# Convolution sums in PSUM, ten adds on GpSimd, and other units cut: a two-layer decoder trunk

## The chip, the cores and the metric

One core of a Trainium2 chip runs the kernel. The metric is the device time of the whole program in microseconds; the median of several executions counts. TensorE multiplies matrices, VectorE (DVE), ScalarE (ACT) and GpSimd (POOL) work element by element, and SyncE (SP) issues DMAs.

## The reference

Two layers on x of 256 tokens by 1024 channels, float32. The first layer, where the change lies:

```python
a, bv, bg, z = jnp.split(h @ w_in, ...)      # 1024, 1024, 1024, 2048 columns
ya = group_matmul(multiscale_pool(a), pool_w) * pool_scale   # windows 2, 4, 8, 16
u = bv * jax.nn.sigmoid(bg)
u = causal_depthwise_conv(u, conv_w, 31 taps) + conv_b
yb = jax.nn.silu(layer_norm(u, cn_g, cn_b))
x = x + (jnp.concatenate([ya, yb], axis=-1) * jax.nn.silu(z)) @ w_out
```

The second layer is attention with 16 heads over the 256 tokens, with per-head norms of queries and keys, and a gated output projection.

## The kernel before

The weights come as 49 units of 1 MiB (128 partitions x 2048 columns), read in order. TensorE takes a unit in one of two ways. A **native** unit is multiplied as it is, in float32. A **split** unit is cut into a high and a low part, and each product becomes three: high by high, low activations, low weights. ScalarE casts the high part (L459, two halves), VectorE subtracts it for the low part (`cut_lo`, L723, two halves). For an **added** unit VectorE does nothing: ScalarE also writes the negated high part (L462), and a GpSimd DMA adds the raw weights to it (`added_low`, L424). Before, units 0, 9, 13, 16, 21, 23 and 25 are native, and 10, 14, 22 and 24 are added.

Units 0 to 7 give gate and value of the convolution in turns, 8 to 11 the four pool groups, 12 to 15 and 17 to 20 the gates z, 16 (`PW`) the pool products with `pool_w`, 21 to 28 the output projection. Units 0 to 15 and 17 to 20 use the PSUM banks 0 to 3 in turn, unit 16 the banks 4 to 7.

The convolution has 31 taps on 8 channel tiles of 256 tokens, taken in four pairs of tiles. A pair's sum stands in `V` in SBUF. ScalarE makes the first tap with the bias (L551). A tap is then either one VectorE operation for each tile (L841, multiply and add), or a **product**: ScalarE multiplies both tiles of the pair (L542, two operations), and VectorE adds the 512 columns (L845). For the first two pairs 14 of the taps go another way (side products): ScalarE multiplies (L518), GpSimd DMAs accumulate in `side_v` (L433), and VectorE adds the two totals at the end (L838).

The order is written out by hand. Each engine's program runs through slots n = 1 to 21; what stands in slot n follows unit n - 1 and prepares the cut of unit n + 2. In VectorE's slot n stand: the gate product of a pair (L876), `cut_lo(n + 2)`, the window sums of pool group n - 9 (L812 to L824), then `taps(n)`. In ScalarE's slot n: the cast of unit n + 2, the products for `taps(n)`, first taps, the gate or copy of unit n, which waits until TensorE has finished it, and side products. The copy of a pool unit (L568) also waits until the window sums before it are done, since they share the buffer `AP`.

Which taps become products, and in which slot, is set by a planner (`conv_plan`). It gives each slot of VectorE and ScalarE 0.95 of a unit's length as time, subtracts the work that is fixed (`slot_work`), and fills the rest with taps. It doesn't know how late an engine really is. Products are kept in a ring of four buffers, and later of four others.

At the end of the first layer the channel mean and the square sum of the layer norm are small matmuls put between output products of unit 23, at `MEAN_AT` and `SUM2_AT` (unit, half, tile). In the second layer ScalarE copies transposed keys and queries out of a bank (`qk_turn_out`, L680), squares them (`qk_squares`, L670), and TensorE transposes the probabilities (`pair_turn`, L1285) into the same bank.

Of the kernel before, what the change touches and what calls it, by code (L numbers as in the profile page):

```python
# [24 lines left out]
S = 256  # L25
# [73 lines left out]
def cut_slot(n):  # L99

    if n == SPARE or n >= Z1[0]:
        return (n - Z1[0]) % 4 if n >= Z1[0] else CUT - 1
    return (cut_index(n) - (n > SPARE) - cut_index(Z1[0]) + 1) % 3

# [6 lines left out]
def slot_free(n):  # L111

    if n == SPARE:
        return released(PW)
# [35 lines left out]
PRODUCTS = 4  # L150
LATE_RING = 4
LATE_SLOT = A[3] + 3

# [5 lines left out]

def side_items(n):  # L160

    return [(pair, n - BG[pair + 1]) for pair in range(SIDE) if 0 <= n - BG[pair + 1] < SIDE_ITEMS]


def product_free(product):

    if product >= LATE_FROM:
        return PRODUCT_USED[product - LATE_RING] if product - LATE_FROM >= LATE_RING else None
    return PRODUCT_USED[product - PRODUCTS] if product >= PRODUCTS else 0


def slot_work(n):

    dve, act = 0, 0.8 * len(side_items(n))
    if n + 2 not in NATIVE and n + 2 not in ADDED and n < OA[0]:
        dve, act = dve + 2.3, act + 1.9
    if n + 3 == SPARE or n + 3 in EARLY_ADDED:
        act += 4.0
    if n - 1 in BV:
        dve, act = dve + 0.6, act + 1.0  # L180
    if n - 1 in A:
        dve += 0.75 * (n - A[0]) + 1.0
    if n - 1 in ZA:
        dve, act = dve + 0.8, act + 0.6
    if n in BG or n in A or n in ZB or n in ZA:
        act += 0.6
    if n in (ZB[0], PW):
        act += 0.7 if n == ZB[0] else 3.2
    return dve, act


def conv_plan():

    plan, last, used, count, before, late, folded = {}, {}, [], 0, None, None, []
    left = {pair: [k for k in range(1, TAPS) if k not in side_taps(pair)] for pair in range(4)}
    folds = [2 * pair + (SIDE_ITEMS + i) % 2 for pair in range(SIDE) for i in range(2)]
    dve_time = act_time = 0.0
    for n in range(BG[1], OA[0] + 1):
# [4 lines left out]
        act_time = min(act_time, ACT_CARRY) + ACT_SHARE * length - act  # L203
        while dve_time > 0 or n == OA[0]:
            here = [pair for pair in left if left[pair] and CONV_PAIRS[pair][0] // 2 < n // 2]
            if not here:
                break
            pair = max(here, key=lambda p: (len(left[p]) - (2 if p == before else 0) - (0 if here == [p] or p < n // 2 - 1 else NEW_LAST), -p))
            before, k, tiles = pair, left[pair].pop(0), CONV_PAIRS[pair]
            if n == LATE_SLOT and late is None:  # L210
                late = len(used)
            free = pair < (n - 1) // 2
            if act_time > 0.8 and free and n < OA[0]:
                count += 1
                plan[n].append((tiles, k, len(used), max(last.get(c, 0) for c in tiles), count))
                used.append(count)
                dve_time, act_time = dve_time - 0.61, act_time - 0.8
# [14 lines left out]
    return plan, last, used, late, folded  # L232
# [3 lines left out]
CONV_PLAN, TILE_DONE, PRODUCT_USED, LATE_FROM, FOLDED = conv_plan()  # L236
# [3 lines left out]
SUM2_AT = 2, 1, 5  # L240
# [3 lines left out]
def hybrid_trunk(nc, xT, w, vec, const, out):  # L244
    with ExitStack() as ctx:
# [100 lines left out]
        first_tap, product_ready, tap = sem("first_tap"), sem("product_ready"), sem("tap")  # L346
        mean_folded = sem("mean_folded")
# [17 lines left out]
        def product_home(product):  # L365

            if product < LATE_FROM:
                b = 2 * (product % PRODUCTS)
                return PR[:, b:b + 2, :]
            i = (product - LATE_FROM) % LATE_RING  # L370
            return (AP, W1, W2)[i][:, :, 0:S] if i < 3 else SG2

        SG2 = SG[:, :].rearrange("p (c t) -> p c t", c=2)

# [32 lines left out]
        def _(pool):  # L407
# [19 lines left out]
            for n in range(BG[1], OA[0]):  # L427
# [7 lines left out]
                if n + 3 in EARLY_ADDED:  # L435
                    added_low(n + 3)
# [13 lines left out]
        def _(act):  # L450
# [70 lines left out]
            for n in range(1, OA[0] + 1):  # L521
# [4 lines left out]
                if n == ZA[0]:  # L526
                    act.wait_ge(tap, PRODUCT_USED[LATE_FROM - 1])
# [6 lines left out]
                for tiles, k, product, _, _ in CONV_PLAN.get(n, ()):  # L534
                    if product is None or k is None:
                        continue
                    if product == LATE_FROM:
# [9 lines left out]
                if n in BG[1:] or n == A[0]:  # L547
                    for c in (n - 2, n - 1):
                        if c == n - 2:
                            act.wait_ge(u_ready, n // 2)  # L550
                        nc.scalar.activation(V[:, c, :], U[:, c, 0:S], ACT.Identity, bias=column(CB + c),  # L551
                                             scale=column(CW + TAPS * c)).then_inc(first_tap, 1)
                if n in BG:
# [5 lines left out]
                for pair, item in side_items(n):  # L559
                    side_product(pair, item)  # L560
                if n in A:
# [14 lines left out]
                if n + 3 in EARLY_ADDED:  # L576
                    cut_hi(n + 3)
# [112 lines left out]
            for octet in range(2):  # L690
                for u, n in enumerate((KU[octet], QU[octet], VU[octet])):
                    for i in range(16):
                        s = 16 * u + i
                        for half in range(2):
                            if s == KT_AT[half]:
# [19 lines left out]
        def _(dve):  # L715
# [111 lines left out]
            def taps(n):  # L827

                for tiles, k, product, ready, _ in CONV_PLAN.get(n, ()):
# [3 lines left out]
                    else:  # L833
                        dve.wait_ge(first_tap, tiles[-1] + 1)
                    if k is None:
                        pair, chain = divmod(product, 2)
                        dve.wait_ge(side_added[pair][chain], 16 * ((SIDE_ITEMS - chain + 1) // 2 - 1))
                        nc.vector.tensor_tensor(V[:, c:c + 2, :], V[:, c:c + 2, :], side_v[:, pair, chain, :, :],  # L838
                                                ALU.add).then_inc(tap, 1)
                    elif product is None:  # L840
                        nc.vector.scalar_tensor_tensor(V[:, c, :], U[:, c, k:k + S], column(CW + TAPS * c + k),  # L841
                                                       V[:, c, :], ALU.mult, ALU.add).then_inc(tap, 1)
                    else:
                        dve.wait_ge(product_ready, product + 1)
                        nc.vector.tensor_tensor(V[:, c:c + 2, :], V[:, c:c + 2, :], product_home(product),  # L845
                                                ALU.add).then_inc(tap, 1)
# [22 lines left out]
            for n in range(1, OA[0] + 1):  # L869
# [9 lines left out]
                if m in A:  # L879
# [7 lines left out]
                taps(n)  # L887
                if n == OA[0]:
                    fold_mean()
                    cut_lo(OA[2], (0,))  # L890
                    centre()
                    cut_lo(OA[2], (1,))
# [4 lines left out]


# [155 lines left out]
        def _(pe):  # L1054
# [102 lines left out]
            for g in range(4):  # L1157
# [3 lines left out]
                if g == 0:  # L1161
                    pe.wait_ge(root_ready, 1)
                for ct in range(2):
# [262 lines left out]
```

## Time and profile before

| | us |
|---|---|
| median of 3 runs | 332.69 (332.54 to 332.81) |
| the profiled execution | 333.14 |
| its span, first to last instruction | 331.3 |

| engine | busy, us | share of the span |
|---|---|---|
| TensorE matmul | 325.0 | 98% |
| VectorE | 256.2 | 77% |
| ScalarE | 230.4 | 70% |
| GpSimd | 51.8 | 16% |

How to read it: busy times are of the whole span. The stretch of the first layer, from 17 to 156 us, is another matter than the mean, and the rows below look into it. TensorE's clock is granted in full in all 40 slices of the page.

### The profile page before, as it was taken

To read this page: it belongs to the slowest core of one execution; us is meant where nothing else is said; L and a number is where in the kernel's file an instruction comes from. 1 tells how busy PE (TensorE), PEld (TensorE's weight loads), DVE (VectorE), ACT (ScalarE), POOL (GpSimd) and SP (SyncE) were. 2 spreads that over 40 slices of the span, in tenths; PEclk is the share of its full clock that TensorE was granted. 3 is DMA by queue.
4 is the path that set the end of the run, shared out by engine and by line. 5 is a ranking of instruction groups with operands and counts; after the bars stand their busy time and mean duration, and the time that the engine had idled before them with its cause. 6 is when DMAs were issued, how large, how long until landed. Compare 5 with 4: busy or idle time off the path is not lost.

```text
span 331.3 us, 5760 instructions
## 1 busy us (share of the span) xinstructions
PE 325.0 (98%) x2212; PEld 296.2 (89%) x2212; DVE 256.2 (77%) x475; ACT 230.4 (70%) x429; POOL 51.8 (16%) x58
## 2 busy tenths in 40 slices
PE   8999999999999999999999999999999999999995
PEld 8899999999989999997999999988887776778885
DVE  2699989999689999996886898747556877748633
ACT  4677999994999897935775557824756666575630
POOL 0050024424422310120000000005500231400000
PEclk9999999999999999999999999999999999999999
DMA  7979488979999998676629343780634323200003
GB/s 277 409 272 357 146 267 217 202 164 349 276 252 345 167 380 296 130 174 208 254 103 403 130 133 133 279 347 10 245 127 166 135 99 132 108 0 2 2 0 127
DMA packets 12842, 64.77 MB, mean 195 GB/s; under 512 B 1424, under 2 KB 1552, under 8 KB 6544
## 3 DMA queue, kind: packets, MB, share of 16 engines
q1 hardware_dynamic: 8064, 53.78, 43.2%
q0 software_dynamic: 4608, 10.49, 17.3%
q8 instruction: 17, 0.28, 0.3%
q10 hardware_dynamic: 144, 0.15, 0.2%
q14 instruction: 9, 0.07, 0.1%
HBM read 52.88 MB, written 1.05 MB: 163 GB/s over the span
## 4 chain that ended last, share of the span: by engine, by line
PE 93%; DMA 3%; ACT 1%; DVE 1%; issue 1%; POOL 0%; ACTq 0%; POOLq 0%
PE bank L1058 25%; PE bank L1060 23%; PE bank L1059 23%; PE bank L1118 5%; PE bank L1092 4%; DMA w_lo<-raw 3%; PE bank L1166 2%; PE bank L1272 2%; PE bank L1299 2%; PE bank L1135 2%; PE bank L1126 2%; PE bank L1285 2%; PE bank L1251 1%; ACT scratch L467 1%; DVE scratch L752 1%
## 5 line engine op out<-in xcount | busy, mean ns | idle before, releaser
L723 DVE TENSOR_TENSOR w_lo<-raw,w_hi 128x1024 fp32r<-128x1024 f32 x76 | 90.3, 1222 | 19.6 <-ACT w_hi L459 19.4
L1058 PE MATMUL bank<-h_hi,w_hi 128*128 128x256 f32 x304 | 86.6, 285 | 0.4 <-DMA w_lo<-raw 0.4
L459 ACT CAST w_hi<-raw 128x1024 fp32r<-128x1024 f32 x84 | 84.4, 1048 | 2.7 <-PE bank L1060 2.7
L1060 PE MATMUL bank<-h_hi,w_lo 128*128 128x256 f32 x304 | 86.0, 283 | 0.0
L1059 PE MATMUL bank<-h_lo,w_hi 128*128 128x256 f32 x304 | 86.0, 283 | 0.0
L1058 PEld LDWEIGHTS bank<-h_hi,w_hi 128*128 128x128 f32 x304 | 58.3, 192 | 0.9 <-issue 0.8
L1059 PEld LDWEIGHTS bank<-h_lo,w_hi 128*128 128x128 f32 x304 | 58.3, 192 | 0.1
L1060 PEld LDWEIGHTS bank<-h_hi,w_lo 128*128 128x128 f32 x304 | 58.3, 192 | 0.0
L841 DVE SCALAR_TENSOR_TENSOR scratch<-scratch,params 128x256 f32<-128x256 f32 x108 | 44.1, 484 | 0.2
L1058 PE MATMUL bank<-w_hi,h_hi 128*128 128x512 f32 x96 | 39.2, 408 | 0.0
L1058 PE MATMUL bank<-ya_hi,w_hi 128*128 128x256 f32 x128 | 38.1, 297 | 0.0
L1060 PE MATMUL bank<-w_hi,h_lo 128*128 128x512 f32 x96 | 37.6, 391 | 0.0
L1059 PE MATMUL bank<-w_lo,h_hi 128*128 128x512 f32 x96 | 37.5, 391 | 0.0
L1060 PE MATMUL bank<-ya_hi,w_lo 128*128 128x256 f32 x128 | 36.1, 282 | 0.0
L1059 PE MATMUL bank<-ya_lo,w_hi 128*128 128x256 f32 x128 | 36.1, 282 | 0.0
L433 POOL DMA_DIRECT2D side_v<-side_ring x24 | 21.1, 908 | 70.8 <-ACT side_ring L518 65.7
L542 ACT ACTIVATE scratch<-scratch,params 128x256 f32<-128x256 f32 x76 | 31.9, 505 | 0.0
L845 DVE TENSOR_TENSOR scratch<-scratch 128x512 f32<-128x512 f32 x38 | 25.7, 692 | 1.4 <-ACT scratch L542 0.2
L1058 PEld LDWEIGHTS bank<-ya_hi,w_hi 128*128 128x128 f32 x128 | 24.4, 191 | 2.0 <-issue 1.7
L1059 PEld LDWEIGHTS bank<-ya_lo,w_hi 128*128 128x128 f32 x128 | 24.5, 191 | 0.1
L1060 PEld LDWEIGHTS bank<-ya_hi,w_lo 128*128 128x128 f32 x128 | 24.4, 191 | 0.0
L444 POOL TENSOR_SCALAR scratch<-scratch 128x8 f32<-128x8 f32 x8 | 4.3, 535 | 122.1 <-DVE scratch L1018 121.9
(106 smaller groups left out, 549.0 us busy)
## 6 DMA issues: line engine op xcount, KB each, us to landing
raw<-w SPq DMA_DIRECT2D x49, 1024.0 KB, 6.3
side_v<-side_ring POOLq DMA_DIRECT2D x24, 256.0 KB, 8.2
w_lo<-raw POOLq DMA_DIRECT2D x8, 512.0 KB, 8.1
X<-xT SPq DMA_DIRECT2D x2, 512.0 KB, 5.2
out<-X SPq DMA_DIRECT2D x4, 256.0 KB, 2.6
consts<-const SPq DMA_DIRECT2D x1, 290.0 KB, 13.5
params<-vec ACTq DMA_DIRECT2D x1, 149.0 KB, 4.9
```

What stands on the lines that cost most here:

```text
L433: pool.dma_start(side_v[:, pair, item % 2, :, :], side_home(pair, item), accum_op=ALU.add).then_inc(side_added[pair][item % 2], 16)
L459: nc.scalar.copy(halves(w_hi, cut_slot(n), half), halves(raw, n % RAW, half)).then_inc(hi_cut, 1)
L542: last = nc.scalar.mul(product_home(product)[:, i, :], U[:, c, k:k + S], column(CW + TAPS * c + k))
L723: nc.vector.tensor_tensor(halves(w_lo, cut_slot(n), half), halves(raw, n % RAW, half), halves(w_hi, cut_slot(n), half).bitcast(F32), ALU.s ...
L841: nc.vector.scalar_tensor_tensor(V[:, c, :], U[:, c, k:k + S], column(CW + TAPS * c + k), V[:, c, :], ALU.mult, ALU.add).then_inc(tap, 1)
L845: nc.vector.tensor_tensor(V[:, c:c + 2, :], V[:, c:c + 2, :], product_home(product), ALU.add).then_inc(tap, 1)
L1058: nc.tensor.matmul(dst, wh, ah, start=start, stop=False, skip_group_check=True)
L1059: nc.tensor.matmul(dst, wh, al, start=False, stop=False, skip_group_check=True)
L1060: return nc.tensor.matmul(dst, wl, ah, start=False, stop=stop, skip_group_check=True)
L1092: last = nc.tensor.matmul(dst, wr, (H if n else H0)[:, k, :], start=start, stop=stop, skip_group_check=True)
L1118: return nc.tensor.matmul(dst, wr, SZ[:, (KD if n in OB else 0) + tile, :], start=start and m % 2 == 0, stop=stop, skip_group_check=True)
L1126: nc.tensor.matmul(bank[7][:, 0:P], ones[:, :], ones[:, :], start=True, stop=True, skip_group_check=True)
```

## The change

- Unit 9 becomes split; it was native. Units 10 and 14 become plain split units, cut by VectorE; they were added. Unit 12 becomes an added unit. With four buffers for cut weights in use from the start (`SLOT_ORDER`), the buffers of the units up to 12 are given out anew.
- VectorE's sums for slots up to 15 stand in PSUM, in banks 4 to 7 (`partial`), not in `V`. ScalarE's first taps go there too.
- GpSimd has sums of its own in `V`. ScalarE starts each of the four with one tap (in slots 3, 5, 7 and 11) and makes ten products for GpSimd, which adds them (`pool_conv`) in its slots 4, 6, 8, 13 and 14, behind a wait for the cut of that slot (`pool_gate`), none in the slots of the pool units.
- In slot 15, behind `cut_lo(17)`, four VectorE adds merge the sums of the banks with those in `V`. TensorE waits for them ahead of unit 16 (`MERGED`). From there on VectorE's sums stand in `V`.
- The products for VectorE fall from 38 to 23, in other ring buffers (`RINGS`), while single taps are 110 for 108.
- In slot 10 the window sums come after the taps; in slot 9 ScalarE makes the added cut of unit 12 ahead of its copy.
- The square sum of the layer norm stands one tile later, `centre` comes after the last low part, and in the second layer ScalarE copies the second half of the keys out before its second square, not after it.

```diff
-NATIVE = frozenset((0, 9, 13, 16, 21, 23, 25))
-EARLY_ADDED = (10, 14)
+NATIVE = frozenset((0, 13, 16, 21, 23, 25))
+EARLY_ADDED = (12,)
...
+FOUR, SLOT_ORDER = ZA[1], (3, 2, 0, 1)
...
-PRODUCTS = 4
-LATE_RING = 4
+RINGS = (0, (1, 2, 3)), (A[0], (2, 3)), (A[1], (3, 4)), (ZB[0], (4,)), (ZB[1], (4, 5, 6, 7))
...
+MERGE_SLOT = PW - 1
...
+POOL_ADDS = {4: (0, 0), 6: (0, 1), 8: (1, 2), 13: (2,), 14: (2, 3, 3)}
+POOL_STARTS = {3: (0,), 5: (1,), 7: (2,), 11: (3,)}
...
+def pool_gate(n):
+
+    if n - 1 in A:
+        return "pooled", n - A[0]
+    return ("cut", 2 * low_cuts(n + 2) + 2) if n + 2 not in NATIVE and n + 2 not in ADDED else None
...
+        for pair in range(4) if n == MERGE_SLOT else ():
+            tiles = CONV_PAIRS[pair]
+            count += 1
+            plan[n].append((tiles, None, None, max(last[c] for c in tiles), count))
...
-SUM2_AT = 2, 1, 5
+SUM2_AT = 2, 1, 6
...
+        def partial(tiles):
+
+            c = tiles[0]
+            at = S * (c % 2)
+            t = bank[4 + c // 2][:, at:at + S * len(tiles)]
+            return t.rearrange("p (c t) -> p c t", c=2) if len(tiles) == 2 else t
...
+            def pool_conv(n):
+
+                gate = pool_gate(n)
+                if gate and POOL_PLAN[n - 1]:
+                    pool.wait_ge(pooled if gate[0] == "pooled" else lo_cut, gate[1])
+                for pair, k, made, ready, _ in POOL_PLAN[n - 1]:
+                    if ready:
+                        pool.wait_ge(pool_tap, ready)
+                    else:
+                        pool.wait_ge(pool_started, 2 * pair + 2)
+                    pool.wait_ge(pool_product, made)
+                    nc.gpsimd.tensor_tensor(V[:, 2 * pair:2 * pair + 2, :], V[:, 2 * pair:2 * pair + 2, :],
+                                            pool_home(made), ALU.add).then_inc(pool_tap, 1)
...
-                    if product_free(product):
-                        act.wait_ge(tap, product_free(product))
+                    if FREE_AT[product]:
+                        act.wait_ge(tap, FREE_AT[product])
...
-                        nc.scalar.activation(V[:, c, :], U[:, c, 0:S], ACT.Identity, bias=column(CB + c),
+                        nc.scalar.activation(partial((c,)), U[:, c, 0:S], ACT.Identity, bias=column(CB + c),
...
                 for t in range(TT):
+                    if isq and t and KT_AT[1] == 32:
+                        qk_turn_out(octet, 0, 1)
...
+                    total = partial(tiles) if done <= MERGED else V[:, c:c + 2, :] if len(tiles) == 2 else V[:, c, :]
+                    if k is None and product is None:
+                        dve.wait_ge(pool_tap, POOL_LAST[c // 2])
+                        nc.vector.tensor_tensor(V[:, c:c + 2, :], total, V[:, c:c + 2, :], ALU.add).then_inc(tap, 1)
...
-                if m in A:
+                if m in A and n + 2 not in EARLY_ADDED:
                     window_sums(m - A[0])
...
                 taps(n)
+                if m in A and n + 2 in EARLY_ADDED:
+                    window_sums(m - A[0])
...
                 if g == 0:
                     pe.wait_ge(root_ready, 1)
+                    pe.wait_ge(tap, MERGED)
```

## Rows read from the trace of the kernel before

**Rows 1.** The page, part 1: engine, busy us (share), instructions; then PEld, DVE, ACT.

```profile
PE 325.0 (98%) x2212; PEld 296.2 (89%) x2212; DVE 256.2 (77%) x475; ACT 230.4 (70%) x429; POOL 51.8 (16%) x58
```

**Rows 2.** TensorE's waits, whole span: waiter, releaser: us in total, times, longest.

```profile
PE bank L1285 <- issue: 0.6, 1, 0.6
PE bank L1135 <- DVE scratch L752: 0.5, 1, 0.5
PE bank L1058 <- DMA w_lo<-raw: 0.4, 1, 0.4
```

**Rows 3.** Chain of waits in order of time: start us, us, what.

```profile
10.30 6.91 PE bank L1092 x32
63.28 6.91 PE bank L1092 x32
...
94.78 0.36 PE bank L1058
106.52 6.91 PE bank L1166 x32
```

**Rows 4.** Timeline of VectorE: start us, us, line, operation, count.

```profile
60.26 0.69 DVE L876 TENSOR_TENSOR scratch<-bank,scratch 128x512 f32<-128x512 f32 x1
...
74.61 1.44 DVE L812 TENSOR_TENSOR scratch<-scratch 128x540 f32<-128x540 f32 x2
...
83.25 2.94 DVE L812 TENSOR_TENSOR scratch<-scratch 128x540 f32<-128x540 f32 x4
...
104.95 2.36 DVE L723 TENSOR_TENSOR w_lo<-raw,w_hi 128x1024 fp32r<-128x1024 f32 x2
...
119.90 1.90 DVE L845 TENSOR_TENSOR scratch<-scratch 128x512 f32<-128x512 f32 x3
...
128.98 4.06 DVE L841 SCALAR_TENSOR_TENSOR scratch<-scratch,params 128x256 f32<-128x256 f32 x10
```

**Rows 5.** Timeline of VectorE: the low parts of units 26 to 28.

```profile
168.86 6.90 DVE L723 TENSOR_TENSOR w_lo<-raw,w_hi 128x1024 fp32r<-128x1024 f32 x6 [0.25 <-ACT w_hi L459]
```

**Rows 6.** Timelines of ScalarE and TensorE in the second layer; idle before, and releaser.

```profile
280.48 0.60 ACT L670 ACTIVATE scratch<-bank 128x512 f32<-128x512 f32 x1 [1.46 <-DVE scratch L1018]
...
281.90 0.85 PE L1285 MATMUL bank<-consts,scratch 128*128 128x128 f32 x6 [0.64 <-issue]
```

**Rows 7.** Groups by shape, 20 to 160 us: busy us, mean ns; idle before.

```profile
L841 DVE SCALAR_TENSOR_TENSOR scratch<-scratch,params 128x256 f32<-128x256 f32 x108 | 44.1, 484 | 0.2
L845 DVE TENSOR_TENSOR scratch<-scratch 128x512 f32<-128x512 f32 x38 | 25.7, 692 | 1.4 <-ACT scratch L542 0.2
L876 DVE TENSOR_TENSOR scratch<-bank,scratch 128x512 f32<-128x512 f32 x4 | 2.8, 688 | 0.0
...
L542 ACT ACTIVATE scratch<-scratch,params 128x256 f32<-128x256 f32 x76 | 31.9, 505 | 0.0
```

**Rows 8.** Timeline of ScalarE: start us, us, line, operation, count, idle before.

```profile
77.14 0.59 ACT L568 COPY scratch<-bank 128x512 f32<-128x512 f32 x1 [2.02 <-DVE scratch L824]
...
81.73 0.59 ACT L568 COPY scratch<-bank 128x512 f32<-128x512 f32 x1 [2.41 <-PE bank L1060]
...
98.56 3.30 ACT L542 ACTIVATE scratch<-scratch,params 128x256 f32<-128x256 f32 x8
...
103.84 1.99 ACT L459 CAST w_hi<-raw 128x1024 fp32r<-128x1024 f32 x2
```

**Rows 9.** Timelines of GpSimd and VectorE.

```profile
17.59 4.55 POOL L415 TENSOR_TENSOR qscale<-consts,params 128x8 f32<-128x8 f32 x1 [16.29 <-DMA consts<-const]
...
280.47 0.24 POOL L444 TENSOR_SCALAR scratch<-scratch 128x8 f32<-128x8 f32 x1 [12.31 <-DVE scratch L1018]
...
283.24 1.16 POOL L444 TENSOR_SCALAR scratch<-scratch 128x8 f32<-128x8 f32 x1 [0.78 <-DVE scratch L1018]
...
283.08 1.23 DVE L723 TENSOR_TENSOR w_lo<-raw,w_hi 128x1024 fp32r<-128x1024 f32 x1
```

**Rows 10.** Busy us by window: stretch, length, PE, PEld, DVE, ACT, POOL; PEclk, DMA, GB/s.

```profile
94.78:100.54 5.76, 5.76 (x48) 5.76 (x49) 5.72 (x13) 5.76 (x15) 1.75 (x2) 1.00 1.06 304
```

More of the change, by code:

```diff
@@ L113, in slot_free @@
     if n == SPARE:
-        return released(PW)
+        return released(max(m for m in CUTS if m <= FOUR and cut_slot(m) == CUT - 1))
     if n == Z1[3]:
@@ L149, with pool_products @@
 SIDE_ITEMS = 14
-PRODUCTS = 4
-LATE_RING = 4
+RINGS = (0, (1, 2, 3)), (A[0], (2, 3)), (A[1], (3, 4)), (ZB[0], (4,)), (ZB[1], (4, 5, 6, 7))
 LATE_SLOT = A[3] + 3
+MERGE_SLOT = PW - 1
+POOL_ADDS = {4: (0, 0), 6: (0, 1), 8: (1, 2), 13: (2,), 14: (2, 3, 3)}
+POOL_STARTS = {3: (0,), 5: (1,), 7: (2,), 11: (3,)}
+def pool_products():
+    plan, starts, taken, count, made, last = {}, {}, {pair: 0 for pair in range(4)}, 0, 0, {}
+    for n in range(BG[1], MERGE_SLOT + 1):
+        for pair in POOL_STARTS.get(n, ()):
+            starts[n] = starts.get(n, ()) + ((pair, FIRST_POOL[pair]),)
+            taken[pair], last[pair] = taken[pair] + 1, 0
+        plan[n - 1] = []
+        for pair in POOL_ADDS.get(n, ()):
+            made, count = made + 1, count + 1
+            plan[n - 1].append((pair, FIRST_POOL[pair] - taken[pair], made, last[pair], count))
+            taken[pair], last[pair] = taken[pair] + 1, count
+    return plan, starts, taken, last
 def side_taps(pair):
     return range(TAPS - SIDE_ITEMS, TAPS) if pair < SIDE else ()
+FIRST_POOL = [TAPS - 1 - (SIDE_ITEMS if pair < SIDE else 0) for pair in range(4)]
+POOL_PLAN, POOL_START, POOL_TAKEN, POOL_LAST = pool_products()
+POOL_USED = [done for items in POOL_PLAN.values() for _, _, _, _, done in items]
+def pool_gate(n):
+    if n - 1 in A:
+        return "pooled", n - A[0]
+    return ("cut", 2 * low_cuts(n + 2) + 2) if n + 2 not in NATIVE and n + 2 not in ADDED else None
 def side_items(n):
     return [(pair, n - BG[pair + 1]) for pair in range(SIDE) if 0 <= n - BG[pair + 1] < SIDE_ITEMS]
[L165 to L169, printed above, removed]
 def slot_work(n):
@@ L192, in conv_plan @@
 def conv_plan():
-    plan, last, used, count, before, late, folded = {}, {}, [], 0, None, None, []
-    left = {pair: [k for k in range(1, TAPS) if k not in side_taps(pair)] for pair in range(4)}
+    plan, last, used, count, before, late, folded, homes, free_at = {}, {}, [], 0, None, None, [], [], []
+    left = {pair: list(range(1, FIRST_POOL[pair] - POOL_TAKEN[pair] + 1)) for pair in range(4)}
     folds = [2 * pair + (SIDE_ITEMS + i) % 2 for pair in range(SIDE) for i in range(2)]
@@ L203, in conv_plan @@
         act_time = min(act_time, ACT_CARRY) + ACT_SHARE * length - act
+        for pair in range(4) if n == MERGE_SLOT else ():
+            tiles = CONV_PAIRS[pair]
+            count += 1
+            plan[n].append((tiles, None, None, max(last[c] for c in tiles), count))
+            dve_time -= 0.61
+            last.update({c: count for c in tiles})
+        if n == MERGE_SLOT:
+            merged = count
         while dve_time > 0 or n == OA[0]:
@@ L216, in conv_plan @@
                 used.append(count)
+                ring = next(homes for first, homes in reversed(RINGS) if n >= first)
+                homes.append(ring[len(homes) % len(ring)])
+                free_at.append(max([u for u, h in zip(used[:-1], homes[:-1]) if h == homes[-1]], default=0))
                 dve_time, act_time = dve_time - 0.61, act_time - 0.8
@@ L231, in conv_plan @@
             last.update({c: count for c in tiles})
-    return plan, last, used, late, folded
+    return plan, last, used, late, folded, merged, homes, free_at
 DVE_SHARE, ACT_SHARE, NEW_LAST, ACT_CARRY = 0.95, 0.95, 40, 1.0
-CONV_PLAN, TILE_DONE, PRODUCT_USED, LATE_FROM, FOLDED = conv_plan()
+CONV_PLAN, TILE_DONE, PRODUCT_USED, LATE_FROM, FOLDED, MERGED, HOMES, FREE_AT = conv_plan()
 MEAN_AT = 2, 0, 1
-SUM2_AT = 2, 1, 5
+SUM2_AT = 2, 1, 6
 EARLY = (BG[0],), (Z1[0], Z1[1])
@@ L425, in added_low, with side_sums @@
                                    accum_op=ALU.add).then_inc(lo_added[i][half], 16)
-            for n in range(BG[1], OA[0]):
+            def side_sums(n):
                 for pair, item in side_items(n):
@@ L526, in _ @@
                 if n == ZA[0]:
-                    act.wait_ge(tap, PRODUCT_USED[LATE_FROM - 1])
+                    act.wait_ge(tap, max(MERGED, PRODUCT_USED[LATE_FROM - 1]))
                 if n - 1 in ZA:
@@ L827, in taps @@
             def taps(n):
-                for tiles, k, product, ready, _ in CONV_PLAN.get(n, ()):
+                for tiles, k, product, ready, done in CONV_PLAN.get(n, ()):
                     c = tiles[0]
```

68 lines of the change are left out of this document (45 added, 23 removed).

## The prediction, made before the change was timed

> **What bounds the kernel now.** I read the busy table first: TensorE is busy for 98% of the span [rows 1], so this kernel ends when TensorE ends, and a change counts only by what it does to TensorE's queue. The waits of TensorE come next: after its start they are 0.6 us ahead of the transposes of L1285, 0.5 us for a square sum and 0.4 us for a low half brought by a GpSimd DMA [rows 2]. Then the chain of waits in order of time: unit 0, native, takes 6.91 us from 10.30; units 1 to 8, split, end at 63.28, which is (63.28 - 17.21) / 8 = 5.76 us each; native unit 9 takes 6.91 again; unit 14 starts at 94.78 and the pool product (unit 16) 2 x 5.76 = 11.52 later, at 106.30 (its row begins at 106.52) [rows 3]. Last, the timelines of VectorE and ScalarE, for how far each runs behind TensorE. VectorE cuts unit 17's low half, the first step of its slot 15, from 104.95 [rows 4]; slot 15 opens when unit 14 is done, at 100.54. So VectorE is 4.4 us late there, which costs nothing before: unit 17 is read only at 106.3 + 6.91 = 113.2.
>
> **What the change takes off TensorE.** Unit 9 split instead of native: 6.91 - 5.76 = 1.15 us less. Unit 14 plain: its DMA wait of 0.42 goes. The square sum one output tile later: of the 0.5 us wait [rows 2] one native product (6.91 / 16 = 0.43) is put in the place. But VectorE starts the low half of unit 26 at 168.86, and the first of its two parts is done 1.2 later, at 170.1 [rows 5]; TensorE asks for it at about 170.3. Being 0.43 earlier against this chain, it would wait some 0.2. I count 0.25. The keys' second copy out (L680) moves ahead of the second square: today ScalarE stands idle 1.46 us before that square and copies after it, and TensorE waits 0.64 for the bank [rows 6]. The two copies (0.40 each, below) fit into the idle time; I count 0.6. Together 2.4 us, as long as nothing new waits.
>
> **Sums of the other engines.** Durations, from start to start: VectorE's 128x256 tap 0.396 ((4.06 - 0.484) / 9), a 512-wide add 0.605 ((1.90 - 0.692) / 2), a cut of one unit 2.3; ScalarE's product half 0.40 ((3.30 - 0.505) / 7) and cast of one unit 1.9 [rows 4, 7, 8]. Walking the plan through both programs gives for VectorE: cuts +4 halves (9, 10, 14 in, 12 out), +4.6; single taps 108 to 110, +0.8; product adds 38 to 23, -9.1; four merges, +2.4: in all 1.3 us less. ScalarE: casts +2 halves, negations -2, product halves 76 to 46, and 20 for GpSimd, and 8 that start its sums: -0.8. Both look relieved. But these sums hide a deadline.
>
> **The new deadline.** VectorE's sums now stand in banks 4 to 7, which unit 16 overwrites. So TensorE waits for the four merges; they stand in slot 15 behind the cut of unit 17. With no earlier stall TensorE reaches unit 16 at 106.30 - 1.15 - 0.42 = 104.7. Slot 15 opens at 98.97, and cut and merges take 2.3 + 2.5 = 4.8 of its 5.76 us: VectorE may be 1 us late there, not 4.4. Behind the waiting matmul stands all the rest of TensorE's queue.
>
> I walk the two queues to that point. Up to slot 7 VectorE loses six adds (-3.6), gets two taps (+0.8), unit 9's cut (+2.3) and 0.8 of waiting for that unit's high half: it starts slot 8 (the gate product, L876) at 60.4 instead of 60.26 [rows 4]. Slot 8: 0.6 + cut 2.3 + 8 taps 3.2, to 66.4. Slot 9: cut 2.3, window sums of pool group 0 1.6, 2 taps 0.8, to 71.1. Slot 10 has no cut any more, but its 8 taps (3.2) stand ahead of the window sums of group 1 (about 2.35, from 74.61 to the copy that they release at 77.14 [rows 4, 8]), which end at 76.7. The copy of unit 10 on ScalarE waits for them, as before, and comes at 76.75 instead of 77.14. (A level of window sums is 2.94 / 4 = 0.73 [rows 4]; hence 1.6 for group 0, 3.1 for group 2, 3.85 for group 3.)
>
> Slot 11 is where it turns. Products 2 and 4 share a buffer. VectorE does the window sums of group 2 first, from 77.4 to 80.5, so product 2 is added by 81.2, and ScalarE can make product 4 only then, where its queue would have had it 2.4 us earlier. It goes on: product 0.8, start of the fourth GpSimd sum 0.8, side products 1.6, and the copy of unit 11 at 84.45. Before, that copy came at 81.73, right behind TensorE [rows 8]. From there ScalarE is never idle: before, its slot 14 products end 101.86 - 81.73 = 20.1 us after this copy [rows 8]; the change takes two negations (2.1) and two products (1.6) out of this stretch, which leaves 16.4: the last product is ready at 100.8, those before it at 0.8 steps. VectorE has by then done cut 14, window sums of group 3 (to 92.1), cut 15 and 8 taps (97.6), so it follows the products: 101.4, 8 taps 104.6, cut of unit 17 106.9, four merges **109.4**. ScalarE's cast of unit 17 starts near 102.8 (103.84 before [rows 8]), in time.
>
> TensorE therefore idles from 104.7 to 109.4, 4.7 us, and unit 16 starts 109.4 - 106.3 = 3.1 us later than before; the 1.15 and 0.42 are inside that difference. Between slot 9 and the merges the two queues wait for TensorE nowhere on this walk, so a late DMA for unit 12 (needed at 80.5) would only move TensorE's idle time. On SyncE's queue the reloads of the raw buffers of units 9 and 10 now wait for VectorE's cuts at 57 and 63, earlier than for the native product's end at 70.2, and the reload for unit 17 waits for unit 13 as before; I count nothing for them. Behind unit 16 ScalarE and VectorE follow TensorE as before, 3.1 us later. Sum: 3.1 - 0.25 - 0.6 = +2.25. From the profiled execution, 333.14 (span 331.3 and 1.8 around it), that is 335.4; it lies 0.45 above the median of 332.69, so **334.9**.
>
> **GpSimd.** No row shows a wide add there. From below it is VectorE's 0.69 [rows 7], from above the 4.55 of its 8-wide product [rows 9]; I take 1.2 to 2, nearer to the lower end, since its 8-wide L444 alone needs only 0.24 [rows 9]. The same L444 takes 1.16 when it falls under a VectorE cut, and ends 0.09 after that cut [rows 9]. So a cut holds GpSimd. The ten adds are gated behind the slot's cut and run beside taps. The last three follow the side DMAs of slot 13, from about 98.7, and the last merge needs them at 108.8: they decide from 3.3 us each. On this walk they cost nothing.
> The Trainium skill (SBUF — State Buffer, "SBUF: two separate sides") lets GpSimd and a VectorE operation with two SBUF inputs lock each other out of a shared port pair, which speaks for sums in PSUM. The 1.16 us row agrees for the one direction.
>
> **VectorE on PSUM.** Its reads cost nothing: 0.688 with a bank as input, 0.692 without [rows 7]. Writes to a bank are in no row. From below: taps as much as 0.1 us faster, which would save 0.8 of the stall in slot 14. From above: each operation holds its successor until it has ended, 0.484 + 0.02 instead of 0.396, 0.11 each; 31 of them lie on the walk (18 up to the window sums of group 1, 13 from the last product), +3.4. I take nothing, by the nearest row.
> The Trainium skill (VectorE: DVE Perf Modes, "The TRN2 errata") gives an operation with its source in PSUM 62 cycles more, 65 ns at 0.96 GHz as an estimate. By it the sum would be 2.0 us higher, 336.9; the 0.688 us row speaks against it.
>
> **The rivals.** (A) The forecast, with TensorE waiting 3.1 to 6.2 us at unit 16: 333.4 to 336.5; 0.50. (B) *Faster*: the relief of 1.3 us and the earlier casts act at once, and the merges are done by 104.7; 332.69 - 2.4 = 330.3. It decides where the walk is 4.7 us too slow. For it: both engines' sums fall. Against: in the 5.76 us from 94.78 VectorE is busy for 5.72 and ScalarE for 5.76 [rows 10], so there is no idle time to take up. 0.17. (C) Product 4 doesn't hold ScalarE in slot 11: the walk is 2.4 shorter, 332.5, no change. The order of the code speaks against it. 0.10. (D) Bank writes hold their successors: +2 to +3.4, 336.9 to 338.3; 0.08. (E) TensorE's granted clock falls in the idle 4.7 us. It is 1.00 [rows 10], the level of 2.4 GHz, in every slice of the page, but the longest wait behind the start is 0.64 [rows 2, 6], so no row tests this. At 1.2 GHz the work behind it takes double; if that holds for a third to a half of unit 16's 6.91, +2.3 to +3.4, about 337.5; 0.12. (F) The change doesn't do what it says, since GpSimd's adds take 4.5 us: 98.7 + 13.6 + 0.7 = 113.0 instead of 109.4, +3.6, 338.5; 0.03.
> On (E) the Trainium skill (TensorE: Matmul & The Clock Gate, "What's actually happening") says that an idle array falls to the lower clock.
>
> **The numbers.** A measurement can tell 0.2% from no change: 332.0 to 333.4. Slower: A 0.50, D 0.08, E 0.12, F 0.03, together 0.73. Same: C, 0.10. Faster: B, 0.17. A's own range is 333.4 to 336.5; to hold 8 in 10 the range takes in C below, and E and most of D above: 331.9 to 338.0. B and F are outside.
>
> **What would show it.** The waits of TensorE led by one of 4.7 us ahead of the pool product, released by a VectorE add; the four merges as one row from about 106.9; the copy of unit 11 near 84.5, behind a ScalarE wait in slot 11; unit 9 at 5.76; no wait ahead of the transposes near 281; GpSimd adds of 1.2 to 2 us; taps at 0.40 from start to start. The prediction is wrong if the merges start before 102.5, or if TensorE's wait is there and something before it made up for it.

## The result, and the profile after

The changed kernel takes 337.40 us (median; 337.22 to 337.83), the kernel before 332.73. The ratio is 1.0141, with a 95% interval of 1.0128 to 1.0154: 4.7 us slower. Direction and place were as forecast, the size was twice the forecast 2.25.

The page of the changed kernel, to be read beside [rows 1]: the line of busy times in tenths and that of the granted clock, 40 slices of 8.4 us each.

```profile
span 335.6 us, 5803 instructions
...
PE   8999999999994999999999999999999999999995
...
PEclk9999999999998799999999999999999999999999
...
L810 DVE TENSOR_TENSOR w_lo<-raw,w_hi 128x1024 fp32r<-128x1024 f32 x80 | 94.9, 1220 | 25.1 <-ACT w_hi L534 24.9
```

TensorE has a hole in slice 13, and behind it, in slices 13 and 14, its clock is granted at 8 and 7 tenths. Before, both lines were full. The span grew by 4.3.

TensorE's waits, over the whole span, against [rows 2]:

```profile
PE bank L1258 <- DVE scratch L925: 4.2, 1, 4.2
PE bank L1217 <- POOL eps L461: 1.0, 1, 1.0
PE bank L1226 <- ACT scratch L542: 0.4, 1, 0.4
PE bank L1149 <- DVE w_lo L810: 0.3, 1, 0.3
PE bank L1149 <- DMA w_lo<-raw: 0.3, 1, 0.3
```

L1258 is the pool product (unit 16), L925 a merge: the new wait is 4.2 us. The wait ahead of the transposes (0.6) is gone, and so is that for the layer norm's square sum (the 0.4 at L1226 is at the start). The DMA that TensorE waits for is now unit 12's, and the 0.3 released by a VectorE cut (L810) is the low part of unit 26.

The chain of waits in order of time, against [rows 3]: start us, us, what.

```profile
9.76 6.91 PE bank L1183 x32
...
104.13 0.81 ACT scratch L617 x2
105.14 1.22 DVE w_lo L810
106.36 2.40 DVE scratch L925 x4
108.90 9.57 PE bank L1258 x32
```

From unit 0 to unit 16 it is 108.90 - 9.76 = 99.1 us, where [rows 3] have 106.3 - 10.3 = 96.0: 3.1 more. And unit 16 itself takes 9.57, not 6.91: 2.66 more. (This execution starts unit 0 half a microsecond earlier, at 9.76. To compare its times below with those of the kernel before, add 0.54.) The two together are 5.76; less the 1.0 that the change saves behind unit 16 (measured alone further down) that is 4.8, against the measured 4.7.

Busy times of TensorE by windows of 2 us: stretch, length, busy (matmuls), granted clock, DMA share, GB/s.

```profile
102.00:104.00 2.00, 2.00 (x19) 1.00 1.03 313
104.00:106.00 2.00, 0.69 (x6) 1.00 1.09 207
106.00:108.00 2.00, 0.00 (x0) 0.75 1.14 210
108.00:110.00 2.00, 1.10 (x3) 0.50 1.07 187
110.00:112.00 2.00, 2.00 (x6) 0.50 0.52 91
112.00:114.00 2.00, 2.00 (x7) 0.55 0.55 95
114.00:116.00 2.00, 2.00 (x11) 1.00 0.22 36
```

TensorE stops at 104.7. During the wait the clock falls to 0.50, the lower of its two levels, 1.2 GHz. It stays there for 5 us of work, in which 6 or 7 matmuls end in 2 us instead of 11, and comes back near 114.

The timelines of VectorE and ScalarE up to there, against [rows 4] and [rows 8]:

```profile
76.77 2.20 DVE L899 TENSOR_TENSOR scratch<-scratch 128x540 f32<-128x540 f32 x3 [0.71 <-ACT scratch L655]
...
97.87 3.10 DVE L935 TENSOR_TENSOR bank<-bank,scratch 128x512 f32<-128x512 f32 x4 [0.80 <-ACT scratch L617]
100.88 3.22 DVE L931 SCALAR_TENSOR_TENSOR bank<-scratch,params,bank 128x256 f32<-128x256 f32 x8
104.00 2.35 DVE L810 TENSOR_TENSOR w_lo<-raw,w_hi 128x1024 fp32r<-128x1024 f32 x2
106.28 2.47 DVE L925 TENSOR_TENSOR scratch<-bank,scratch 128x512 f32<-128x512 f32 x4
```

```profile
76.15 0.59 ACT L655 COPY scratch<-bank 128x512 f32<-128x512 f32 x1 [2.21 <-DVE scratch L911]
76.63 1.71 ACT L617 ACTIVATE scratch<-scratch,params 128x256 f32<-128x256 f32 x4
80.61 0.91 ACT L617 ACTIVATE scratch<-scratch,params 128x256 f32<-128x256 f32 x2 [2.27 <-DVE bank L935]
...
83.83 0.56 ACT L655 COPY scratch<-bank 128x512 f32<-128x512 f32 x1
```

ScalarE makes two products at 76.63, waits 2.27 for VectorE to take the first out of the shared buffer, and makes the third at 80.61; the copy of unit 11 follows at 83.83. VectorE gets the products of slot 14 from 97.87, cuts unit 17 at 104.00 and merges from 106.28.

### The profile page after: what moved, and what is told of

Read it like the earlier page. It is cut to its first block, busy times and chain, and to the rows that moved or that the text cites. A ratio compares the mean times of both kernels' runs of the same rounds, so it can differ in the third digit from the quotient of the medians.

```text
span 335.6 us, 5803 instructions
## 1 busy us (share of the span) xinstructions
PE 325.5 (97%) x2228; PEld 296.8 (88%) x2228; DVE 253.4 (76%) x470; ACT 229.2 (68%) x427; POOL 62.3 (19%) x66
## 4 chain that ended last, share of the span: by engine, by line
PE 74%; DVE 12%; ACT 10%; DMA 1%; issue 1%; ACTq 0%; DVEq 0%
PE bank L1149 20%; PE bank L1151 19%; PE bank L1150 19%; DVE bank L931 3%; PE bank L1258 3%; DVE w_lo L810 3%; ACT side_ring L593 2%; PE bank L1209 2%; ACT w_hi L534 2%; PE bank L1183 2%; PE bank L1364 2%; PE bank L1391 2%; PE bank L1226 2%; PE bank L1377 2%; DMA X<-xT 1%; ACT scratch L617 1%
## 5 line engine op out<-in xcount | busy, mean ns | idle before, releaser
L810 DVE TENSOR_TENSOR w_lo<-raw,w_hi 128x1024 fp32r<-128x1024 f32 x80 | 94.9, 1220 | 25.1 <-ACT w_hi L534 24.9
L1149 PE MATMUL bank<-h_hi,w_hi 128*128 128x256 f32 x320 | 91.2, 285 | 0.3 <-DMA w_lo<-raw 0.3
L1150 PE MATMUL bank<-h_lo,w_hi 128*128 128x256 f32 x320 | 90.5, 283 | 0.0
L1151 PE MATMUL bank<-h_hi,w_lo 128*128 128x256 f32 x320 | 90.5, 283 | 0.0
L1149 PEld LDWEIGHTS bank<-h_hi,w_hi 128*128 128x128 f32 x320 | 61.4, 192 | 0.5 <-issue 0.4
L1150 PEld LDWEIGHTS bank<-h_lo,w_hi 128*128 128x128 f32 x320 | 61.4, 192 | 0.1
L1151 PEld LDWEIGHTS bank<-h_hi,w_lo 128*128 128x128 f32 x320 | 61.4, 192 | 0.0
L931 DVE SCALAR_TENSOR_TENSOR bank<-scratch,params,bank 128x256 f32<-128x256 f32 x76 | 30.8, 482 | 0.1
L1149 PEld LDWEIGHTS bank<-w_hi,h_hi 128*128 128x128 f32 x96 | 18.0, 188 | 5.6 <-issue 2.3
L1209 PE MATMUL bank<-scratch,raw 128*128 128x256 f32 x96 | 21.5, 379 | 0.0
```

What stands on the lines that cost most here:

```text
L810: nc.vector.tensor_tensor(halves(w_lo, cut_slot(n), half), halves(raw, n % RAW, half), halves(w_hi, cut_slot(n), half).bitcast(F32), ALU.s ...
L931: nc.vector.scalar_tensor_tensor(total, U[:, c, k:k + S], column(CW + TAPS * c + k), total, ALU.mult, ALU.add).then_inc(tap, 1)
L1149: nc.tensor.matmul(dst, wh, ah, start=start, stop=False, skip_group_check=True)
L1150: nc.tensor.matmul(dst, wh, al, start=False, stop=False, skip_group_check=True)
L1151: return nc.tensor.matmul(dst, wl, ah, start=False, stop=stop, skip_group_check=True)
L1209: return nc.tensor.matmul(dst, wr, SZ[:, (KD if n in OB else 0) + tile, :], start=start and m % 2 == 0, stop=stop, skip_group_check=True)
```

## The experiments

The theory after the result has three parts: the merges come late because both queues lag (unit 16 starts 3.1 us later than before); the lag's last 2.3 us come from the shared product buffer; and the idle wait costs a second time, since TensorE's clock falls. Times are medians; each ratio is to the kernel before on the same chip.

### Is it the clock that makes unit 16 longer?

```diff
                 if g == 0:
                     pe.wait_ge(root_ready, 1)
+                    pe.wait_ge(sz_ready, 1)
+                    for _ in range(9):
+                        nc.tensor.matmul(bank[0][:, 0:S], ones[:, :], H0[:, 0, :], start=True, stop=True,
+                                         skip_group_check=True)
                     pe.wait_ge(tap, MERGED)
```

> The changed kernel with nine extra native products (about 3.9 us of TensorE work, result not used) into bank 0 inside TensorE's 4.2 us wait ahead of unit 16. Theory (clock): the 2.7 us that unit 16 takes over its 6.91 come from the granted clock, which fell during the idle wait; kept busy, TensorE runs unit 16 in 6.9 us at a clock of 1.00, and the time falls by 2.7, from 337.4 to 334.7. Rival (something else slows unit 16, such as VectorE and ScalarE at PSUM beside it or the reading of the weights): unit 16 still takes 9.6 us and the time stays at 337.4. In both the wait for the merges ends at the same moment, near 108.9.

Measured: 335.03 us (334.89 to 335.08), ratio 1.0074 (1.0059 to 1.0089). Its timeline of TensorE:

```profile
105.25 4.05 PE L1256 MATMUL bank<-scratch,ones 128*128 128x256 f32 x18
109.13 7.07 PE L1262 MATMUL bank<-scratch,raw 128*128 128x256 f32 x32
```

Its chain of waits has unit 16 as

```profile
109.30 6.91 PE bank L1262 x32
```

More work for TensorE, and 2.4 us less time. Its clock is 1.00 in every window from 102 to 116, and unit 16 takes 6.91 in the chain, where it took 9.57. (Where nothing is waited for, a timeline begins the row of a native unit 0.17 earlier than the chain and counts 7.07 for the same 6.91; behind a wait both views agree.) The 0.3 that lack to the expected 2.7 are its start, 109.30 instead of 108.90: in this execution TensorE waited 1.0 for the DMA of unit 12, so the nine products ended a little behind the merges. The rival, that the neighbours slow unit 16, falls: they all still run.

With four products, which leave half of the wait idle:

```diff
-                    for _ in range(9):
+                    for _ in range(4):
```

> The changed kernel with four extra native products (1.7 us, result not used) at the start of the 4.2 us wait, so that 2.4 us of it stay idle. The merges still end near 108.9. Clock theory, from the two kernels with an idle wait of 2: the clock falls in some executions and not in others, so times from 334.9 (as with nine products) to about 337, wider apart than with nine. Rival (any idle wait costs the full 2.7): 337.4 in all.

Measured: 335.54 (334.83 to 336.72), ratio 1.0088 (1.0068 to 1.0109).

```profile
105.00 1.89 PE L1256 MATMUL bank<-scratch,ones 128*128 128x256 f32 x8
108.97 8.86 PE L1262 MATMUL bank<-scratch,raw 128*128 128x256 f32 x32 [2.08 <-DVE scratch L925]
```

An idle wait of 2.08 us was enough in this execution to make unit 16 take 8.86. The clock didn't fall in the wait here, but behind it: in windows of 0.4 us it is 1.00 up to 110.0 and 0.50 from 110.4 on, more than 1 us into unit 16. Nor does it fall in every execution. Each has a mean granted clock on record; for the kernel before it is 0.997 to 1.00. Here it is 0.993 to 0.995 in three of the four, with spans of 333.6 to 334.9 us, and 1.00 in the fourth, with a span of 333.0 and a time of 334.83, that of nine products.

### Does the wait hang on VectorE's order?

The merges ahead of the cut of unit 17:

```diff
-                if n < OA[0]:
+                if n < OA[0] and n != MERGE_SLOT:
                     cut_lo(n + 2)
...
+                if n == MERGE_SLOT:
+                    taps(n, True)
+                    cut_lo(n + 2)
                 taps(n)
```

> The changed kernel with the four merges of slot 15 ahead of the cut of unit 17 on VectorE. Theory: the wait is the lag of VectorE's queue; the merges end 2.27 us earlier, TensorE waits 1.9 instead of 4.2. With so short a gap the clock theory has the granted clock stay at 1.00: 337.4 - 2.3 - 2.7 = 332.4. If the extra time of unit 16 doesn't hang on the length of the wait: 337.4 - 2.3 = 335.1. Rival (the merges wait for GpSimd's last adds, which end near 101.7 in the trace, or for something else than VectorE's queue): 337.4.

Measured: 333.55 (332.60 to 334.45 in 10 runs), ratio 1.0023 (1.0009 to 1.0037).

```profile
106.66 8.83 PE L1263 MATMUL bank<-scratch,raw 128*128 128x256 f32 x32 [2.05 <-DVE scratch L927]
```

The wait is 2.05 instead of 4.2, as expected, and the cut that came 2.4 later (at 106.43) held nobody. The other half of the expectation held only in part: in the profiled execution the clock fell also with a wait of 2.05 (8.83 for unit 16), again only when TensorE was back at work, as its windows show (length, busy, granted clock, DMA share, GB/s):

```profile
106.00:108.00 2.00, 1.34 (x6) 1.00 1.11 202
108.00:110.00 2.00, 2.00 (x6) 0.51 1.09 196
```

In three of the ten executions the mean granted clock is 0.995, and these three have the longest spans, 331.9 to 332.7. In the other seven it is 0.998 or more, and the spans are 330.8 to 331.4; the lowest time, 332.60, is near the 332.4 expected for a clock that stays. Two times of this group, 333.88 and 334.04, are long for another reason: their spans are 330.9 us, and 3.0 and 3.1 us lie outside of the span, where it is 1.8 in most executions.

### Does the lag come from the shared buffer?

The third product of slot 11 gets a buffer of its own, one of GpSimd's four that is free then:

```diff
+            if product == OWN:
+                return PR[:, 2:4, :]
...
+                    if product == OWN:
+                        act.wait_ge(pool_tap, POOL_USED[4])
-                    if FREE_AT[product]:
+                    elif FREE_AT[product]:
                         act.wait_ge(tap, FREE_AT[product])
...
+                    if made == 9:
+                        act.wait_ge(tap, PRODUCT_USED[OWN])
```

> The changed kernel with a buffer of its own for the third product of slot 11 (it shared one with the first). Theory: ScalarE's 2.3 us wait in slot 11 goes, everything behind it in both queues comes 2.3 us earlier up to the merges, TensorE waits about 1.9, and the clock stays: 332.4. Rival (VectorE, not ScalarE, sets the pace from slot 12 on, so that the time freed in slot 11 is waited elsewhere): merges end within 0.5 us of before, 337.4, or in between if it is part of it: 335.1 to 337.

Measured: 333.33 (332.68 to 336.07), ratio 1.0033 (1.0011 to 1.0055). The timelines of ScalarE, VectorE and TensorE:

```profile
76.61 2.50 ACT L624 ACTIVATE scratch<-scratch,params 128x256 f32<-128x256 f32 x6
...
81.42 0.56 ACT L664 COPY scratch<-bank 128x512 f32<-128x512 f32 x1
```

```profile
103.87 2.47 DVE L934 TENSOR_TENSOR scratch<-bank,scratch 128x512 f32<-128x512 f32 x4
```

```profile
106.49 8.83 PE L1267 MATMUL bank<-scratch,raw 128*128 128x256 f32 x32 [1.92 <-DVE scratch L934]
```

The three products now stand in one row. The copy of unit 11 comes 2.41 earlier, and the merges, 22 us later, start 2.41 earlier: everything between the two is handed on without loss. Behind the rest of the wait, 1.92, the clock again fell in the profiled execution, near 107.2; by the mean granted clock (0.994 and 0.995, elsewhere 0.997 or more) it did so in two of the ten.

### Both together

> Both edits together: merges ahead of the cut, and a buffer of its own. Theory: the merges end 4.5 us earlier, near 104.2, when TensorE reaches unit 16 at 104.4: no wait, clock 1.00, and the time is 337.4 - 4.2 - 2.7 = 330.5, some 2.2 below the kernel before (332.7), which is what the change takes off TensorE. Rival (the two don't add up, or a wait moves to units 17 to 21, for the low part of unit 17 comes 2.5 us later): 331.5 to 333.

Measured: 330.91 (330.33 to 332.42), ratio 0.9958 (0.9944 to 0.9972): faster than the kernel before by 1.6 us. The merges start at 101.91, TensorE has no wait ahead of unit 16, and the unit takes its 7.07 by the timeline (the row below), which is 6.91 in the chain.

```profile
104.89 7.07 PE L1272 MATMUL bank<-scratch,raw 128*128 128x256 f32 x32
```

So the change's own gains were there all the time, behind the wait and the clock.

### Where does the spread of these kernels come from?

Merges first, with four extra products in the wait:

> The merges ahead of the cut, and the 2.0 us that TensorE still waits filled with four extra native products (1.7 us, result not used). If the spread of that kernel (332.6 to 334.45) is the clock falling in some executions, this one stays at its lowest, 332.6 within 0.3, in all of them, with unit 16 at 6.9 us. Rival (the spread has another cause, such as the DMAs): the same spread, median 333.5.

Measured: 333.09 (332.46 to 335.35), ratio 1.0020 (1.0003 to 1.0036). Not as the theory had it: the profiled execution has its clock at 1.00 throughout, yet its time, 333.17, is not the lowest, and the times spread by 2.9 us. One execution of the ten, the slowest, has a mean granted clock of 0.992 (span 333.5); the other nine have 0.997 or more, and their spans still go from 330.7 to 332.1. So the clock is only a part of the spread. This is the wait in its timeline that was 0.17 in the kernel without the products:

```profile
81.27 0.35 PE L1154 MATMUL bank<-h_hi,w_hi 128*128 128x256 f32 x1 [1.22 <-DMA w_lo<-raw]
```

Unit 12, the added one, is late: its low half comes by a GpSimd DMA that took 11 us here, 10 in the others. In the changed kernel such a delay costs nothing, since the merges set unit 16's start (in the kernel with nine products unit 12 was 1.0 late, and the merges began at 106.24 as ever); once they are early, it counts (and the four products, which then start late, add to it). Hence one more edit on the kernel with both: ScalarE cuts unit 12 ahead of slot 9's side products, and GpSimd issues its DMAs ahead of theirs.

```diff
+                if n + 3 in EARLY_ADDED:
+                    cut_hi(n + 3)
                 for pair, item in side_items(n):
                     side_product(pair, item)
-                if n + 3 in EARLY_ADDED:
-                    cut_hi(n + 3)
```

> The kernel with both edits, and unit 12's added cut moved ahead of the side products of slot 9 on ScalarE, its two DMAs ahead of the side DMAs on GpSimd: their issue comes 1.6 us earlier. Theory: the spread of the kernel with both edits (330.33 to 332.42) is TensorE waiting for that low part, 0.3 in its profile and 1.2 in the profile of the kernel with merges first and four products; with 1.6 us more the wait goes, the median is 330.4 and the spread under 0.8. Rival (the spread has another cause, or the side sums' DMAs now crowd the same transfer): median 330.9 as before, spread 2.

Measured: 330.41 (330.23 to 331.49, five of the six up to 330.60), ratio 0.9938 (0.9926 to 0.9950). All that TensorE still waits for:

```profile
PE bank L1231 <- POOL eps L466: 1.0, 1, 1.0
PE bank L1240 <- ACT scratch L547: 0.4, 1, 0.4
PE bank L1163 <- DVE w_lo L819: 0.3, 1, 0.3
```

The expected median came. The expected spread, under 0.8, holds for the spans, which are 328.4 to 328.8 where the kernel with both edits had 328.5 to 330.6; the one time of 331.49 has 1.0 us more outside its span. The DMA took as long as before (10.2 us for 10.3); what helped is the earlier issue, at 68.6 instead of 70.4. Of the 0.5 by which the two profiled executions differ, 0.2 is unit 0's start (9.87 for 10.06), which the edit doesn't touch. This is the fastest kernel of the study, 2.2 us below the kernel before (332.57 on this chip) and about 7 below the change as it was.

### The parts by themselves

The two edits late in the kernel, made on the kernel before:

```diff
-SUM2_AT = 2, 1, 5
+SUM2_AT = 2, 1, 6
...
+                    if isq and t and KT_AT[1] == 32:
+                        qk_turn_out(octet, 0, 1)
...
-                            if s == KT_AT[half]:
+                            if s == KT_AT[half] != 32:
```

> The kernel before with two edits of the change alone: the square sum one tile later, and the keys' second copy ahead of the second square. The prediction counted 0.25 + 0.6 = 0.85 for them: 332.6 - 0.85 = 331.7, and TensorE's waits of 0.5 ahead of the square sum and 0.6 ahead of the transposes gone from the trace. Rival (the time is handed on, the low part of unit 26 or the second square being late instead): 332.3 to 332.6, with a new wait behind either place.

Measured: 331.69 (331.55 to 331.90), ratio 0.9970 (0.9958 to 0.9981), so 1.0 us less for the counted 0.85. TensorE's waits at L1285 and at the square sum are gone. As the prediction feared, one is handed on: TensorE now waits 0.33 for the low part of unit 26 (forecast 0.2).

The change of units alone, without sums in PSUM and adds on GpSimd:

```diff
-NATIVE = frozenset((0, 9, 13, 16, 21, 23, 25))
-EARLY_ADDED = (10, 14)
+NATIVE = frozenset((0, 13, 16, 21, 23, 25))
+EARLY_ADDED = (12,)
```

> The kernel before with the change of units alone: 9 split, 10 and 14 plain, 12 added; no sums in PSUM, no adds on GpSimd. VectorE has 4.6 us more of cuts, and the planner leaves 28 single taps for slot 21 where it left 14, +5.5 us ahead of the channel mean, which had 1.4 us of slack and gets TensorE 1.6 us earlier. Theory (VectorE's load is what GpSimd had to take over): TensorE waits some 3 to 5 us for the mean, 332.6 - 1.6 + 4 = 335, and up to 2 to 3 more if the clock falls there. Rival (VectorE's idle time of 3.7 us at 89 and ScalarE's relief take it up): no new wait, 331.0.

Measured: 337.66 (336.73 to 338.69), ratio 1.0149 (1.0127 to 1.0171). Its timeline of VectorE, TensorE's wait, and two windows (stretch, length, busy of PE, PEld, DVE, ACT, POOL, granted clock, DMA share, GB/s):

```profile
139.11 11.17 DVE L841 SCALAR_TENSOR_TENSOR scratch<-scratch,params 128x256 f32<-128x256 f32 x28
```

```profile
PE bank L1181 <- DVE scratch L858: 4.6, 1, 4.6
```

```profile
152.00:154.00 2.00, 1.03 (x3) 0.89 (x4) 0.79 (x2) 0.00 (x0) 0.00 (x0) 0.68 0.22 80
154.00:156.00 2.00, 2.00 (x6) 1.64 (x5) 1.81 (x4) 1.03 (x2) 0.00 (x0) 0.50 0.00 0
```

VectorE pays the cuts with 28 taps at the end, TensorE waits 4.6 us for the channel mean, and the clock falls to 0.50 again, at another place. The time is that of the theory with the clock's fall (337 to 338). So the cuts do need the relief that the rest of the change gives VectorE, and the drop of the clock is not bound to unit 16. Which share of that relief is GpSimd's adds and which the fewer products was not taken apart.

### What GpSimd's adds cost, and what the gates are for

```diff
-                gate = pool_gate(n)
-                if gate and POOL_PLAN[n - 1]:
-                    pool.wait_ge(pooled if gate[0] == "pooled" else lo_cut, gate[1])
```

> The changed kernel without GpSimd's gates: its adds start when their product is there, also beside VectorE's cuts. Theory from the 1.16 us row of before: a cut (two SBUF inputs) and a GpSimd add shut each other out; some adds last 2 us and more instead of 1.27, or cuts more than 1.23, while taps and adds on a bank keep 0.48 and 0.69. Adds that come early cost at most a cut or two held up by 1.3 us, in slots 3 to 8, where ScalarE sets the pace: time 337.4 within 0.5, up to 339 if the hold is handed on to the merges. Rival (no mutual hold): all adds 1.2 to 1.3, all cuts 1.22, the time 337.4.

Measured: 340.91 (340.37 to 341.28), ratio 1.0244 (1.0229 to 1.0259): 3.5 us slower than with the gates, and 1.9 above the most that was expected. The timelines of GpSimd and VectorE, and VectorE's groups by shape from 20 to 112 us (busy us, mean ns), of this kernel:

```profile
47.98 2.88 POOL L497 TENSOR_TENSOR scratch<-scratch 128x512 f32<-128x512 f32 x2
...
60.28 2.94 POOL L497 TENSOR_TENSOR scratch<-scratch 128x512 f32<-128x512 f32 x2
```

```profile
48.98 4.10 DVE L807 TENSOR_TENSOR w_lo<-raw,w_hi 128x1024 fp32r<-128x1024 f32 x2
...
61.37 4.08 DVE L807 TENSOR_TENSOR w_lo<-raw,w_hi 128x1024 fp32r<-128x1024 f32 x2
```

```profile
L807 DVE TENSOR_TENSOR w_lo<-raw,w_hi 128x1024 fp32r<-128x1024 f32 x26 | 34.9, 1381 | 3.3 <-ACT w_hi L531 3.3
L928 DVE SCALAR_TENSOR_TENSOR bank<-scratch,params,bank 128x256 f32<-128x256 f32 x76 | 30.8, 479 | 0.1
```

A cut of one unit takes 4.1 us beside two adds instead of 2.35, and one window sum took 2.68 instead of 0.71; taps on a bank keep their 0.479. The adds get longer too, with a median of 1.66 for 1.30, though none takes the expected 2. The hold goes both ways, as the Trainium skill has it (SBUF — State Buffer, "SBUF: two separate sides"). The expectation had the mechanism right and its price wrong, for the delay is handed on: TensorE's wait for the merges is 6.8 us, of which 2.6 are new. Unit 12's DMA is waited for 0.4 longer, and unit 16 takes 9.76, 0.2 more. With these the span grows by 3.2; what is left of the 3.5 isn't in the profiled span.

## Why the prediction was right and wrong

**The bound and the way to it** were right: TensorE's queue decides, and the new wait ahead of unit 16 is the largest, 4.2 us.

**The walk** held at each of its stations (0.54 to be added to the trace's times). Window sums of group 1 released the copy of unit 10 at 76.15, forecast 76.75; the wait for the shared buffer 2.27, forecast 2.4; the copy of unit 11 at 83.83, forecast 84.45; the cut of unit 17 at 104.00, forecast 104.6; the merges from 106.28 to 108.75, forecast 106.9 to 109.4. Unit 16 started 3.1 later, as forecast. The wait itself was 4.2 and not 4.7, since TensorE came later to it: 0.3 of the difference is the wait for unit 12's DMA, which the prediction said would only move TensorE's idle time. One sum in it is off without consequence: its terms up to slot 7 (-3.6, +0.8, +2.3, +0.8) give 60.56 and not 60.4 for the start of slot 8; the trace has 60.37, with the 0.54 added. The kernel with the buffer of its own shows that slot 11 was indeed where it turned.

**The gains** were right in size: 1.0 measured alone for the 0.85 of the two late edits, with a wait of 0.33 at unit 26 where 0.2 was forecast. For units 9 and 14 it counted 1.57; in the fastest kernel unit 16 starts 94.5 us after unit 0, where it was 96.0.

**PSUM and GpSimd**: taps on a bank took 0.482 and adds on a bank 0.695, like those in SBUF, so the value taken (nothing) was right. The 62 cycles that the Trainium skill gives (VectorE: DVE Perf Modes, "The TRN2 errata") are not there: merges, with a bank as source, have a mean of 0.678. GpSimd's adds took 1.29 to 1.74, inside the 1.2 to 2.

**The step that failed** is case (E). The prediction noted that TensorE would stand idle for 4.7 us, longer than any wait in the trace of before, and that no row showed what its clock does then; it then let the clock stay, gave its fall 0.12, and took 334.9. The fall came, in the changed kernel and in each profiled execution of this study in which TensorE stood idle for 1.9 us or more, though not in each execution of the kernels with about 2 us. In the changed kernel it cost 2.66 (counted in (E): 2.3 to 3.4). With that term the sum is 334.9 + 2.7 = 337.6, measured 337.4. The weighing was the fault: the silence of a trace without long waits is no evidence that the clock would stay, and case (E) itself said that no row tested it. It should have been the likeliest case, once the wait was forecast at 4.7.
The Trainium skill (TensorE: Matmul & The Clock Gate, "What's actually happening") has an idle array fall to the lower clock: by that rule the forecast would have been 337.5, and the trace agrees for the wait of 4.2; behind the waits of about 2 the fall came only with TensorE back at work.

**Rivals.** (A), the wait without the clock, had the wait (4.2, in its 3.1 to 6.2), but its times end at 336.5. (B) was not so, but the kernels with early merges show that its time, 330.3, was what lay behind the wait (330.4). (C) named the right place, and the code's order decided it. (D) and (F) were not so.

## What to carry to other kernels

A deadline that a change adds (here: sums moved into banks that the bound engine will need) is to be held against how late the other engines run at that place, not against their totals: VectorE had less work (253.4 us busy for 256.2) and came 4.2 too late. An idle wait on TensorE is to be counted twice, once for its length and once for the clock behind it (at 4 us in every execution here, at 2 us in a part of them); filling it with work that nobody needs gave back 2.4 of 4.7 us, and taking away the lag (one buffer, one step of order) gave back all. GpSimd's adds beside VectorE are cheap only while VectorE works on PSUM.

## What the runs showed of the hardware

- TensorE's granted clock fell to 0.50 in waits of 4.2, 4.6 and 6.8 us, in all executions of these kernels (mean granted clock 0.989 to 0.994). With waits of 1.9 to 2.1 us it fell in three of ten, two of ten and three of four executions, and in the three profiled ones it fell when TensorE was already back at work, 0.7 to 1.4 us into unit 16, which then took 8.83 to 8.86 for 6.91.
- A VectorE operation with two SBUF inputs and a GpSimd add hold each other up: a cut of 2.35 took 4.1, and the median add 1.66 for 1.30. Operations that have one of their two inputs in a bank were not held (taps 0.479, adds 0.690).
- VectorE's writes to a bank cost the same as to SBUF (0.482 and 0.695 against 0.484 and 0.692).
- A GpSimd DMA that adds 512 KB of weights landed after 4.6 to 13.2 us within one kernel; for unit 12, whose DMA took about 10, TensorE waited 0.2 to 1.2 in different profiled executions, and not at all once it was issued 1.6 us earlier.
